# Mixing the two branches of a layer in place in the PSUM banks, on one core

## The chip, the cores and the metric

One core of one Trainium2 chip runs the whole program in one launch. The metric is the device time of an execution in microseconds (us); of several runs the median is given. TensorE is the matmul engine (PE), VectorE is DVE, ScalarE is ACT, GpSimd is POOL, and SyncE (SP) issues most DMAs.

## The reference, cut to what matters

The program is two transformer-like blocks of two layers each, on 512 tokens of width 1024, in fp32. Only the first block is touched. In each of its two layers the outputs of an attention branch and of a gated delta-rule branch are mixed with two gates and sent through one more projection:

```python
y_attn = grid_attention(qa, ka, va) @ w_o_attn[l]
...
y_dn = o.reshape(b, s, DN_V).astype(x.dtype) @ w_o_dn[l]
gates = jax.nn.sigmoid(gate_logit).reshape(b, s, N_BRANCH, D_MODEL)
mixed = gates[:, :, 0] * y_attn + gates[:, :, 1] * y_dn
x = x + (mixed @ w_out[l]).astype(x.dtype)
h = rmsnorm(x, norm_ffn_g[l])
```

## The kernel before, in words

Activations lie transposed: a tile is 128 channels by 512 tokens, and a matrix of width 1024 is 8 such tiles (KB = 8). A product is computed by `gemm_pe` (line 310) in output tiles, one PSUM bank each, banks 0 to 3 in turn, so a product of 8 output tiles takes two turns. fp32 accuracy comes from three matmuls per pair of blocks (lines 343 to 345): weight high part times activation high part, weight high times activation low, weight low times activation high. The high part is the value rounded to the narrower format, the low part is the rest. So each activation tile has to be split in two before TensorE may read it: ACT writes the high part (`h_hi_act`, line 458), DVE subtracts it from the value for the low part (`h_lo_dve`, line 461). The weights are split by POOL (`split_weights`, lines 294 and 296), four slabs in flight (`SLOTS`), each slab being the weights of one output tile. SP (`gemm_sp`, line 228) loads the next slab of a slot when the bank that used the slot is full, by the semaphore `bank_full`. TensorE waits for a slab by `slab_split` and for its bank by `bank_free`.

The order of the work is written out by hand: each engine has its own list, and semaphores join them. With `late=True` the first turn of a product is staggered (line 321): all but the last two activation tiles for output tile 0, then the same for output tile 1, then the last two for both, then output tiles 2 and 3 whole. With `ready` given, TensorE waits ahead of activation tile k of output tile 0 until its low part is there (line 340).

The stage that the change touches is `gates_pe`, `gates_act` and `gates_dve` (lines 1676 to 1738). It has two products back to back:

- the delta branch's output projection: 8 output tiles, each from 4 activation tiles (12 matmuls per bank)
- the projection by `w_out`: 8 output tiles, each from 8 activation tiles (24 matmuls per bank), whose input is the mixed tiles

Between them stands the mixing. The gated output of the attention branch already lies in `H` (8 tiles in SBUF, multiplied by its gate on POOL, line 1666). ACT has turned the delta gates into sigmoids in `ARENA`, tiles 10 to 17 (line 1713). DVE then takes each bank k of the first product as it becomes full: it multiplies it by the gate into the SBUF tile `KF` and frees the bank (line 1732), then adds `KF` to tile k of `H` (line 1735). ACT writes the high part of each finished `H` tile. Only after all 8 tiles does DVE write the 8 low parts into `H_LO` (`h_lo_dve`, line 463). The second product waits for these, tile by tile. Behind it stands `model_dve` (line 465), which adds each bank to `X` (line 483) and prepares the next product.

These lines say the order that matters:

```python
                    nc.vector.tensor_tensor(KF[:], BANK[nb][:], A(i * 4 + (10 + nb)), MUL
                                            ).then_inc(bank_free[nb], 1)
                    dve.wait_ge(bank_free[nb], need(bank_free[nb]))
                    nc.vector.tensor_tensor(blk(H, i * 4 + nb), blk(H, i * 4 + nb), KF[:], ADD).then_inc(mixed_ready, 1)
                    dve.wait_ge(mixed_ready, need(mixed_ready))
            for k in range(KB):
                h_lo_dve(dve, k, tile_of(H_LO), mixed_hi)
```

Of the kernel before, what the change touches and what calls it, by code (L numbers as in the profile page):

```python
# [17 lines left out]
KB = D_MODEL // P  # L18
# [44 lines left out]
def build(nc, w_k8, w_k12, w_k10, xT, memT, par, cst, even, odd, outT, scratch, gate_rows, x_rows):  # L63
    F, R = mybir.dt.float32, mybir.dt.float32r
    ALU, ACT, AX = mybir.AluOpType, mybir.ActivationFunctionType, mybir.AxisListType
    MUL, ADD, SUB = ALU.mult, ALU.add, ALU.subtract
    ctx = ExitStack()
    with ctx:
        def sb(name, shape, dtype=F):
            return ctx.enter_context(nc.sbuf_tensor(name, shape, dtype))  # L70

        def views(*parts):

            with ExitStack() as shared:
                return [shared.enter_context(nc.sbuf_tensor(name, [P, n], R)) for name, n in parts]
# [5 lines left out]
        H_LO, = views(("H_LO", KB * SEQ))  # L81
        H = sb("H", [P, KB * SEQ])
# [12 lines left out]
        QF, KF, VF = sb("QF", [P, SEQ]), sb("KF", [P, SEQ]), sb("VF", [P, SEQ])  # L95
# [16 lines left out]
        BANK = [PSUM[:, b * SEQ:(b + 1) * SEQ] for b in range(8)]  # L112

        def A(i, n=SEQ):
            return ARENA[:, bass.ds(i * SEQ, n)]

        def blk(t, i, n=SEQ, w=SEQ):
            return t[:, bass.ds(i * w, n)]
# [26 lines left out]
        h_hi, h_split = sem("h_hi"), sem("h_split")  # L145
        bank_full = [sem(f"bank_full{b}") for b in range(4)]
        bank_free = [sem(f"bank_free{b}") for b in range(4)]
        squares_added, out_done = sem("squares_added"), sem("out_done")
        sq_done, ss_done, rt_done = sem("sq_done"), sem("ss_done"), sem("rt_done")
        dve_step, act_step, pool_step = sem("dve_step"), sem("act_step"), sem("pool_step")  # L150
# [7 lines left out]
        mixed_ready = sem("mixed_ready")  # L158
# [8 lines left out]
        attn_gates, dn_gates = sem("attn_gates"), sem("delta_gates")  # L167
# [37 lines left out]
        taken = {}  # L205
# [104 lines left out]
        def gemm_pe(pe, slabs, rhs, kb=KB, n=SEQ, halves=False, ready=None, between=None, norm=False, late=False):  # L310

            need = need_pe
            base = need.seen.get(ready.name, 0) if ready is not None else 0

            def parts_of(s):
                return [(s, 2 * (s % 2), 0, kb // 2), (s, 2 * (s % 2) + 1, kb // 2, kb)] if halves else [(s, s, 0, kb)]

            def staggered():
                head = [(s, 2 * s, 0, kb // 2) if halves else (s, s, 0, kb - 2) for s in range(2)]
                tail = [(s, 2 * s + 1, kb // 2, kb) if halves else (s, s, kb - 2, kb) for s in range(2)]
                return head + tail

            def turn(count, between=None, norm=False, late=False):
                order = (staggered() if late else []) + [part for s in range(2 if late else 0, count) for part in parts_of(s)]
                for s, b, k0, k1 in order:
                    first = 0 if not halves or b % 2 == 0 else kb // 2
                    if k0 == 0:  # L330
                        pe.wait_ge(slab_split[s], need(slab_split[s]))
                        need.skip(slab_in[s], 16)
                    if k0 == first:
                        pe.wait_ge(bank_free[b], need(bank_free[b]))
                    out = BANK[b][:, 0:n]
                    final = kb // 2 if halves and b % 2 == 0 else kb
                    for k in range(k0, k1):
                        w_hi, w_lo = (t[s][:, k * P:(k + 1) * P] for t in (W_HI, W_LO))
                        if s == 0 and ready is not None:
                            pe.wait_ge(ready, base + k + 1)  # L340
                        if s == 0 and norm and k == kb - 1:
                            model_sums_pe(pe)
                        mm(out, w_hi, rhs[0](k), start=k == first, stop=False)  # L343
                        mm(out, w_hi, rhs[1](k), start=False, stop=False)  # L344
                        last = mm(out, w_lo, rhs[0](k), start=False, stop=k == final - 1)  # L345
                    if k1 == final:
                        last.then_inc(bank_full[b], 1)
                    if k1 == kb:
                        if s == 1 and norm:
                            model_rows_pe(pe)  # L350
                        if between is not None:
                            between(s)

            per = {bank_free[b]: 2 if halves else 1 for b in range(4)} | {slab_in[s]: 16 for s in range(SLOTS)} | \
                {slab_split[s]: 1 for s in range(SLOTS)}
            whole = slabs // SLOTS
            if between is not None:
                for first in range(0, whole * SLOTS, SLOTS):
                    turn(SLOTS, lambda s: between(first + s), norm and first == 0)
            else:  # L360
                if norm or late or whole == 1:
                    turn(SLOTS, norm=norm, late=late)
                    whole -= 1
                if whole:
                    with need.loop(pe, whole, per):
                        turn(SLOTS)
                turn(slabs % SLOTS)
            if ready is not None:
                need.skip(ready, kb)

        def rhs_of(t, n=SEQ, first=0):
            return lambda k: t[:, (first + k) * n:(first + k + 1) * n]
# [85 lines left out]
        def h_hi_act(k, hi, x=None):  # L458
            nc.scalar.activation(hi(k), x(k) if x else blk(H, k), ACT.Copy).then_inc(h_hi, 1)

        def h_lo_dve(dve, k, lo, hi, x=None):
            dve.wait_ge(h_hi, need_dve(h_hi))
            nc.vector.tensor_tensor(lo(k), x(k) if x else blk(H, k), hi(k).bitcast(F), SUB).then_inc(h_split, 1)  # L463
# [49 lines left out]
        def tile_of(t):  # L513
            return lambda k: blk(t, k)
# [519 lines left out]
        delta_l = [None]  # L1034
# [641 lines left out]
        def gates_pe(pe):  # L1676
            need = need_pe
            taken[f"gates{delta_l[0]}"] = [need.seen[bank_free[b].name] + 1 for b in range(4)]
            gemm_pe(pe, 8, (lambda k: branch_hi(4 + k), lambda k: branch_lo(4 + k)), kb=4, ready=h_split, late=True)
            gemm_pe(pe, 8, (mixed_hi, rhs_of(H_LO)), ready=h_split, late=True)  # L1680
            taken[f"out{delta_l[0]}"] = [need.seen[bank_free[b].name] + 1 for b in range(4)]

        def gates_back_sp(sp, l):
# [15 lines left out]
        def branch_hi(k):  # L1699
            return blk(H_LO2, k)  # L1700

        def mixed_hi(k):
            return blk(ACT_HI, 10 + k) if k < 2 else blk(ACT_LO, k - 2)

        def branch_lo(k):
            return blk(ACT_HI, k if k < 4 else 2 + k)

        def gates_act(act):
            for k in range(4, KB):
                h_hi_act(k, branch_hi, branch)  # L1710
            for i in range(4):
                act.wait_ge(gate_in[i], 16 * (delta_l[0] + 1))
                nc.scalar.activation(A(10 + 2 * i, 2 * SEQ), A(10 + 2 * i, 2 * SEQ), ACT.Sigmoid).then_inc(dn_gates, 1)
            skip_banks(need_act, 2)
            for k in range(KB):
                act.wait_ge(mixed_ready, need_act(mixed_ready))
                h_hi_act(k, mixed_hi)
            skip_banks(need_act, 2)

        def gates_dve(dve, l):  # L1720
            need = need_dve
            for k in range(4, KB):
                h_lo_dve(dve, k, branch_lo, branch_hi, branch)
            banks_taken(dve, need, f"gates{l}")
            dve.wait_ge(*nth("gated", 1))
            per = {bank_full[b]: 1 for b in range(4)} | {bank_free[b]: 1 for b in range(4)} | {mixed_ready: 4, dn_gates: 2}
            with need.loop(dve, 2, per) as i:
                for nb in range(4):
                    dve.wait_ge(bank_full[nb], need(bank_full[nb]))
                    if nb % 2 == 0:  # L1730
                        dve.wait_ge(dn_gates, need(dn_gates))
                    nc.vector.tensor_tensor(KF[:], BANK[nb][:], A(i * 4 + (10 + nb)), MUL
                                            ).then_inc(bank_free[nb], 1)
                    dve.wait_ge(bank_free[nb], need(bank_free[nb]))
                    nc.vector.tensor_tensor(blk(H, i * 4 + nb), blk(H, i * 4 + nb), KF[:], ADD).then_inc(mixed_ready, 1)
                    dve.wait_ge(mixed_ready, need(mixed_ready))
            for k in range(KB):
                h_lo_dve(dve, k, tile_of(H_LO), mixed_hi)


        GT, UP = [QF, KF], [VF, KTOK]
# [1591 lines left out]
```

## Time and profile before

| what | value |
|---|---|
| median of 3 runs | 3731.81 us (3726.59 to 3734.32) |
| the profiled execution's own time | 3725.19 us |
| its span, first to last instruction | 3723.4 us |
| mean granted TensorE clock over the span | 0.975 of full |
| busy: PE, POOL, DVE, ACT | 3585.1, 1818.3, 1694.3, 986.7 us |

The times in the rows further down are microseconds from the start of the span, of one execution. A row of the timeline gives start, duration, engine, line, operation, output and inputs, count, and in brackets how long the engine had been idle and whose result ended that. Matmuls are pipelined, so a row's duration is longer than the distance to the next start; it is the distance that counts. The granted clock is 1.00 at full speed (2.4 GHz) and 0.50 at the lower level (1.2 GHz).

### The profile page before, as it was taken

What the parts mean: (1) busy time and instruction counts of PE and PEld (TensorE: products, weight loads), DVE (VectorE), ACT (ScalarE), POOL (GpSimd) and SP (SyncE); (2) the same over time, 40 slices, a digit from 0 to 9 for tenths busy, and PEclk for the clock granted to TensorE, in tenths of its full rate; (3) what the DMA queues carried; (4) which work ended last, traced back from release to release, by engine and by line L of the source; (5) the groups of instructions that cost most, each with busy time, mean ns of one, the idle gap of its engine ahead of it and who ended that gap; (6) DMA issues with size and microseconds to landing.
All of it is one profiled execution on the core that took longest, in us unless ns stands there. A gap on an engine that the chain in (4) does not pass through costs nothing.

```text
span 3723.4 us, 49812 instructions
## 1 busy us (share of the span) xinstructions
PE 3585.1 (96%) x18732; PEld 2866.8 (77%) x18732; DVE 1694.3 (46%) x2646; ACT 986.7 (26%) x1742; POOL 1818.3 (49%) x1057
## 2 busy tenths in 40 slices
PE   7999889999999989999999999999999999999999
PEld 5777667878776767787878788888887789888887
DVE  5255645637434573573651254344344124344342
ACT  3235532201223464221111233232111124232010
POOL 5522335656553223666666433535656431435654
PEclk9999899999999989999999999999999999999999
DMA  3221022323222101222222311212223423213222
GB/s 117 90 71 32 13 79 81 103 78 98 87 96 97 52 1 58 90 96 91 96 91 92 100 41 52 80 60 93 100 90 102 102 85 97 79 51 96 96 90 91
DMA packets 84152, 299.18 MB, mean 80 GB/s; under 512 B 8600, under 2 KB 9752, under 8 KB 83608
## 3 DMA queue, kind: packets, MB, share of 16 engines
q1 hardware_dynamic: 81904, 290.11, 23.9%
q10 hardware_dynamic: 1032, 2.62, 0.6%
q0 software_dynamic: 1056, 4.19, 0.4%
q8 instruction: 115, 1.88, 0.2%
q14 instruction: 45, 0.37, 0.0%
HBM read 285.88 MB, written 11.01 MB: 80 GB/s over the span
## 4 chain that ended last, share of the span: by engine, by line
PE 80%; DVE 9%; ACT 4%; issue 3%; DMA 2%; POOL 1%; DVEq 0%; ACTq 0%; SPq 0%; POOLq 0%
PE PSUM L345 19%; PE PSUM L344 19%; PE PSUM L343 19%; PE PSUM L904 2%; PE PSUM L1929 1%; PE PSUM L905 1%; PE PSUM L906 1%; PE PSUM L1933 1%; DVE PSUM L502 1%; DMA SLABS<-w_k 1%; PE PSUM L959 1%; DVE ACT_HI L1820 1%; PE PSUM L1501 1%; PE PSUM L916 1%; PE PSUM L1409 1%
## 5 line engine op out<-in xcount | busy, mean ns | idle before, releaser
L296 POOL TENSOR_TENSOR W_LOS<-SLABS,W_HI 128x1024 fp32r<-128x1024 f32 (+3 forms) x454 | 1142.1, 2516 | 37.9
L294 POOL TENSOR_SCALAR W_HI<-SLABS 128x1024 fp32r<-128x1024 f32 (+3 forms) x454 | 507.6, 1118 | 1299.7 <-DMA SLABS<-w_k 1299.6
L344 PE MATMUL PSUM<-H_LO,W_HI 128*128 128x512 f32 x2480 | 984.5, 397 | 0.0
L343 PE MATMUL PSUM<-H_HI,W_HI 128*128 128x512 f32 x2224 | 883.4, 397 | 27.9 <-DVE H_LO L487 22.0
L345 PE MATMUL PSUM<-H_HI,W_LOS 128*128 128x512 f32 x2224 | 884.7, 398 | 0.0
L344 PEld LDWEIGHTS PSUM<-H_LO,W_HI 128*128 128x128 f32 x2480 | 469.0, 189 | 118.1 <-issue 2.4
L343 PEld LDWEIGHTS PSUM<-H_HI,W_HI 128*128 128x128 f32 x2224 | 419.0, 188 | 133.1 <-issue 21.9
L345 PEld LDWEIGHTS PSUM<-H_HI,W_LOS 128*128 128x128 f32 x2224 | 418.7, 188 | 98.7
L502 DVE TENSOR_TENSOR PSUM<-PSUM,FACTORS 128x512 f32<-128x512 f32 x282 | 195.2, 695 | 555.8 <-PE PSUM L345 493.4
L343 PE MATMUL PSUM<-ACT_HI,W_HI 128*128 128x512 f32 x928 | 370.9, 400 | 19.0 <-DVE H_LO L463 12.3
L345 PE MATMUL PSUM<-ACT_HI,W_LOS 128*128 128x512 f32 x928 | 372.0, 401 | 0.0
L344 PE MATMUL PSUM<-ACT_LO,W_HI 128*128 128x512 f32 x896 | 356.6, 398 | 0.0
L343 PEld LDWEIGHTS PSUM<-ACT_HI,W_HI 128*128 128x128 f32 x928 | 176.4, 190 | 63.5 <-issue 11.0
L345 PEld LDWEIGHTS PSUM<-ACT_HI,W_LOS 128*128 128x128 f32 x928 | 176.6, 190 | 41.9
L344 PEld LDWEIGHTS PSUM<-ACT_LO,W_HI 128*128 128x128 f32 x896 | 169.8, 190 | 42.9 <-issue 0.2
L483 DVE TENSOR_TENSOR X<-PSUM,X 128x512 f32<-128x512 f32 x72 | 49.7, 690 | 208.7 <-PE PSUM L345 208.7
L410 DVE TENSOR_TENSOR X<-PSUM,X 128x512 f32<-128x512 f32 x40 | 27.6, 691 | 248.3 <-PE PSUM L345 248.3
L431 ACT ACTIVATE H_HI<-X,PARAM 128x512 fp32r<-128x512 f32 x64 | 45.6, 723 | 267.7 <-DVE X L483 267.7
L904 PE MATMUL PSUM<-H_HI,W_HI 128*128 128x512 f32 x256 | 108.5, 424 | 0.0
L1801 DVE SCALAR_TENSOR_TENSOR QF<-PSUM,PARAM,QF 128x511 f32<-128x511 f32 (+1 forms) x88 | 65.9, 749 | 88.2 <-ACT QF L1771 42.5
L906 PE MATMUL PSUM<-H_HI,W_LOS 128*128 128x512 f32 x256 | 102.7, 401 | 0.0
L905 PE MATMUL PSUM<-H_LO,W_HI 128*128 128x512 f32 x256 | 102.5, 400 | 0.0
(503 smaller groups left out, 5003.2 us busy)
## 6 DMA issues: line engine op xcount, KB each, us to landing
SLABS<-w_k SPq DMA_DIRECT2D x406, 512.0 KB, 3.5
SLABS<-w_k SPq DMA_DIRECT2D x32, 768.0 KB, 4.2
SLABS<-w_k SPq DMA_DIRECT2D x32, 640.0 KB, 3.9
X<-xT SPq DMA_DIRECT2D x2, 2048.0 KB, 9.7
X<-w_k SPq DMA_DIRECT2D x2, 2048.0 KB, 9.1
SLABS<-w_k SPq DMA_DIRECT2D x16, 256.0 KB, 3.2
ARENA<-gate_rows SPq DMA_DIRECT2D x8, 512.0 KB, 5.2
bias_rows<-SQ ACTq DMA_DIRECT2D x1, 2560.0 KB
```

The source lines that it names most:

```text
L294: nc.gpsimd.tensor_scalar(hi, raw, 1.0, 0.0, MUL, ADD).then_inc(pool_step, 1)
L296: nc.gpsimd.tensor_tensor(lo, raw, hi.bitcast(F), SUB).then_inc(slab_split[s], 1)
L343: mm(out, w_hi, rhs[0](k), start=k == first, stop=False)
L344: mm(out, w_hi, rhs[1](k), start=False, stop=False)
L345: last = mm(out, w_lo, rhs[0](k), start=False, stop=k == final - 1)
L431: nc.scalar.activation(hi(k), blk(X, k), ACT.Copy, scale=G(gain, k)).then_inc(h_hi, 1)
L483: nc.vector.tensor_tensor(xb, BANK[k % 4][:], xb, ADD).then_inc(bank_free[k % 4], 1)
L502: nc.vector.tensor_tensor(BANK[b][:], BANK[b][:], FACTORS[:], MUL).then_inc(scaled, 1)
L904: mm(BANK[b][:], hi, blk(H_HI, i), start=i == 0, stop=False)
L905: mm(BANK[b][:], hi, blk(H_LO2, i), start=False, stop=False)
L906: last = mm(BANK[b][:], lo, blk(H_HI, i), start=False, stop=i == KB - 1)
L1801: last = nc.vector.scalar_tensor_tensor(buf[:, lo:hi], BANK[b][:, lo + o:hi + o], G(conv, col), buf[:, lo:hi], MUL, ADD)
```

## The change

The mixing is done in place in the PSUM bank, and the low part of a tile is written by DVE one tile behind, out of the bank, inside the same list. The bank is freed by the low part and no longer by the gate product. TensorE's wait ahead of each activation tile of the second product is on the `bank_free` count that the low part raises, not on `h_split`. ACT reads the high part out of the bank. `KF` is no longer used here, the mixed tiles are no longer written to `H`, and DVE's loop of two turns is unrolled into 8 tiles. DMAs, weights, matmuls and their order are the same.

```diff
@@ gemm_pe
-            base = need.seen.get(ready.name, 0) if ready is not None else 0
+            base = need.seen.get(ready.name, 0) if ready is not None and not callable(ready) else 0
...
-                        if s == 0 and ready is not None:
+                        if s == 0 and callable(ready):
+                            pe.wait_ge(*ready(k))
+                        elif s == 0 and ready is not None:
                             pe.wait_ge(ready, base + k + 1)
...
-            if ready is not None:
+            if ready is not None and not callable(ready):
                 need.skip(ready, kb)
@@ gates_pe
-            gemm_pe(pe, 8, (mixed_hi, rhs_of(H_LO)), ready=h_split, late=True)
+            gemm_pe(pe, 8, (mixed_hi, rhs_of(H_LO)), ready=mixed_split, late=True)
@@
+        def mixed_split(k):
+            return bank_free[k % 4], taken[f"gates{delta_l[0]}"][k % 4] + 1 + k // 4
+
@@ gates_act
-                h_hi_act(k, mixed_hi)
+                h_hi_act(k, mixed_hi, lambda k: BANK[k % 4][:])
@@ gates_dve
-            per = {bank_full[b]: 1 for b in range(4)} | {bank_free[b]: 1 for b in range(4)} | {mixed_ready: 4, dn_gates: 2}
-            with need.loop(dve, 2, per) as i:
-                for nb in range(4):
-                    dve.wait_ge(bank_full[nb], need(bank_full[nb]))
-                    if nb % 2 == 0:
-                        dve.wait_ge(dn_gates, need(dn_gates))
-                    nc.vector.tensor_tensor(KF[:], BANK[nb][:], A(i * 4 + (10 + nb)), MUL
-                                            ).then_inc(bank_free[nb], 1)
-                    dve.wait_ge(bank_free[nb], need(bank_free[nb]))
-                    nc.vector.tensor_tensor(blk(H, i * 4 + nb), blk(H, i * 4 + nb), KF[:], ADD).then_inc(mixed_ready, 1)
-                    dve.wait_ge(mixed_ready, need(mixed_ready))
+
+            def low(k):
+                dve.wait_ge(h_hi, need(h_hi))
+                nc.vector.tensor_tensor(blk(H_LO, k), BANK[k % 4][:], mixed_hi(k).bitcast(F), SUB).then_inc(bank_free[k % 4], 1)
+
             for k in range(KB):
-                h_lo_dve(dve, k, tile_of(H_LO), mixed_hi)
+                bank = BANK[k % 4][:]
+                dve.wait_ge(bank_full[k % 4], need(bank_full[k % 4]))
+                if k % 2 == 0:
+                    dve.wait_ge(dn_gates, need(dn_gates))
+                nc.vector.tensor_tensor(bank, bank, A(10 + k), MUL).then_inc(dve_step, 1)
+                dve.wait_ge(dve_step, need(dve_step))
+                nc.vector.tensor_tensor(bank, bank, blk(H, k), ADD).then_inc(mixed_ready, 1)
+                if k:
+                    low(k - 1)
+            low(KB - 1)
+            for b in range(4):
+                need.seen[bank_free[b].name] = taken[f"gates{l}"][b] + 2
```

## Rows read from the trace of the kernel before

**Rows 1.** The page: span, busy time by engine, and the chain's shares by engine.

```profile
span 3723.4 us, 49812 instructions
PE 3585.1 (96%) x18732; PEld 2866.8 (77%) x18732; DVE 1694.3 (46%) x2646; ACT 986.7 (26%) x1742; POOL 1818.3 (49%) x1057
PE 80%; DVE 9%; ACT 4%; issue 3%; DMA 2%; POOL 1%; DVEq 0%; ACTq 0%; SPq 0%; POOLq 0%
```

**Rows 2.** TensorE's waits, whole span: total us, times, longest us.

```profile
PE PSUM L343 <- DVE H_LO L463: 14.6, 6, 5.1
```

**Rows 3.** Timeline of TensorE at the seam of the two products, layer 0.

```profile
545.95 0.40 PE L345 MATMUL PSUM<-H_LO,W_LOS 128*128 128x512 f32 x1
...
550.85 0.40 PE L345 MATMUL PSUM<-H_LO,W_LOS 128*128 128x512 f32 x1
556.33 0.77 PE L343 MATMUL PSUM<-ACT_HI,W_HI 128*128 128x512 f32 x1 [5.09 <-DVE H_LO L463]
...
567.23 0.45 PE L343 MATMUL PSUM<-ACT_HI,W_HI 128*128 128x512 f32 x1
567.52 0.40 PE L344 MATMUL PSUM<-H_LO,W_HI 128*128 128x512 f32 x1
```

**Rows 4.** Timeline of TensorE at the same seam, layer 1.

```profile
1505.89 0.40 PE L345 MATMUL PSUM<-H_LO,W_LOS 128*128 128x512 f32 x1
1511.43 0.77 PE L343 MATMUL PSUM<-ACT_HI,W_HI 128*128 128x512 f32 x1 [5.14 <-DVE H_LO L463]
...
1523.37 0.39 PE L343 MATMUL PSUM<-ACT_HI,W_HI 128*128 128x512 f32 x1
```

**Rows 5.** The chain of waits in that stretch, layer 0: start, us, what.

```profile
551.40 0.70 DVE KF L1732
552.24 2.52 DVE H L1735
554.95 8.23 DVE H_LO L463 x4
```

**Rows 6.** Busy time by stretch: PE, PEld, DVE, ACT, POOL, granted clock, DMA.

```profile
544.00:551.00 7.00, 7.00 (x32) 5.49 (x30) 4.61 (x5) 1.37 (x3) 6.83 (x6) 1.00 0.64 201
...
551.00:567.00 16.00, 8.73 (x20) 5.50 (x19) 13.82 (x10) 2.65 (x4) 11.38 (x6) 0.58 0.12 41
...
567.00:615.00 48.00, 48.00 (x204) 37.98 (x203) 22.88 (x25) 10.07 (x16) 28.37 (x16) 1.00 0.28 88
```

**Rows 7.** The three DVE operations of the mixing: ns min/median/max, both layers.

```profile
L1732 DVE TENSOR_TENSOR KF<-PSUM,ARENA x16: 690/692/693, 532.8 to 1506.4; 128x512 f32<-128x512 f32 x16
L1735 DVE TENSOR_TENSOR H<-H,KF x16: 692/1103/2550, 533.6 to 1507.3; 128x512 f32 x16
L463 DVE TENSOR_TENSOR H_LO<-H,ACT_LO x12: 676/678/2851, 558.9 to 1520.0; 128x512 fp32r<-128x512 f32 x12
```

**Rows 8.** Operations elsewhere with a PSUM operand: ns min/median/max.

```profile
L502 DVE TENSOR_TENSOR PSUM<-PSUM,FACTORS x282: 683/698/700, 41.4 to 3653.7; 128x512 f32<-128x512 f32 x141
L483 DVE TENSOR_TENSOR X<-PSUM,X x72: 680/692/692, 573.2 to 3342.9; 128x512 f32<-128x512 f32 x72
L442 ACT ACTIVATE FACTORS<-PSUM x10: 597/598/601, 40.6 to 3356.7; 128x512 f32<-128x512 f32 x10
```

**Rows 9.** Timeline of POOL: low parts of the second product's first weight slabs.

```profile
547.61 2.71 POOL L296 TENSOR_TENSOR W_LOS<-SLABS,W_HI 128x1024 fp32r<-128x1024 f32 x1
...
551.86 2.34 POOL L296 TENSOR_TENSOR W_LOS<-SLABS,W_HI 128x1024 fp32r<-128x1024 f32 x1
...
555.73 2.67 POOL L296 TENSOR_TENSOR W_LOS<-SLABS,W_HI 128x1024 fp32r<-128x1024 f32 x1
...
1502.70 2.71 POOL L296 TENSOR_TENSOR W_LOS<-SLABS,W_HI 128x1024 fp32r<-128x1024 f32 x1
```

**Rows 10.** Timeline of DVE and of ACT at the first mixed tile, layer 0.

```profile
528.57 3.90 ACT L1713 ACTIVATE ARENA<-ARENA 128x1024 f32<-128x1024 f32 x4
...
532.78 0.69 DVE L1732 TENSOR_TENSOR KF<-PSUM,ARENA 128x512 f32<-128x512 f32 x1 [4.49 <-PE PSUM L345]
```

## The prediction

> **What bounds the kernel now.** I began with the page: TensorE is busy 3585.1 of 3723.4 us and holds 80% of the chain that ended last [rows 1]. So time comes off only where TensorE stands still or runs slowly, and the question for any edit of DVE's or ACT's work is whether TensorE waits for it. The list of TensorE's waits says yes: it waited 6 times, 14.6 us in all, 5.1 us at the longest, for the low parts of line 463, the form that the change moves [rows 2].
>
> Then the timeline at the seam of the two products. In steady state TensorE starts 21 matmuls between 545.95 and 550.85, which is 4.90 / 21 = 0.2333 us for one [rows 3]. The last matmul of the first product starts at 550.85, so the next could start at 551.09. It starts at 556.33, released by the low part of tile 0 [rows 3]. The chain shows what lies between: gate product 0.70 us, addition 2.52 us, then four low parts in 8.23 us, of which TensorE takes each as it comes [rows 5]. And there is a second loss behind the wait: the granted clock was 1.00 up to the seam, 0.58 from 551 to 567 and 1.00 after it [rows 6]. The clock is at the full level before TensorE stands still, falls towards the lower one (1.2 GHz) with it, and comes back only when 18 matmuls have gone.
>
> **What this costs, step by step.** Layer 0: the 20th matmul of the second product starts at 567.52 [rows 3]. Without wait and at full rate it would start at 551.09 + 19 x 0.2333 = 555.52. The difference is 12.0 us: 5.24 of standing still ahead of the first matmul, 10.90 for the first 18 where 4.20 would do (6.70), and 0.06 at the last. Layer 1: the last matmul of the first product is at 1505.89, the next could be at 1506.13; the 22nd of the second product starts at 1523.37 [rows 4], and could start at 1506.13 + 21 x 0.2333 = 1511.03. The difference is 12.3 us. Together 24.3 us is all that this seam holds.
>
> **What the change does, part by part.**
>
> *The low parts move into the tile's own turn.* DVE then has three operations per tile: gate product, addition, low part of the tile before. Their prices: the gate product today reads PSUM and one SBUF tile and takes 690 to 693 ns in all 16 cases [rows 7]. Written back into the bank, its nearest row is line 502, PSUM from PSUM and SBUF, 698 ns (683 to 700, 282 times) [rows 8]. The in-place addition has these same kinds of operands, 698 ns. The low part becomes SBUF from PSUM and one SBUF tile, the form of line 483 and of today's gate product, 692 ns [rows 7, 8]. From the start of a gate product to the addition that needs it there is 0.84 us (551.40 to 552.24) [rows 5]; the other two follow without a fresh result to wait for. A tile costs 0.84 + 0.70 + 0.69 = about 2.2 us. TensorE fills a bank in 12 x 0.2333 = 2.8 us. DVE keeps up, and its low parts hide beside the matmuls of the next bank.
>
> *These prices have an upper bound in today's rows.* The addition of line 1735 has two SBUF inputs and takes 692 ns at best, 1103 in the middle, 2550 at worst; the low parts 676 to 2851 [rows 7]. In 551 to 567, where they are slow, POOL is busy 11.38 of 16 us with the weights [rows 6]. The gate product, with one SBUF input, never left 693 ns in the same stage. After the change no DVE operation of this stage has two SBUF inputs. I take the low end, because operands and place match; the high end is in a rival. The Trainium skill has a rule for it (SBUF — State Buffer, "Who interferes with whom"): a DVE instruction with two SBUF inputs contends with a GpSimd instruction that reads SBUF, one with at most one SBUF input doesn't. The rows so far agree, and by that rule the high end can't come.
>
> *A rule that speaks against it.* Reading PSUM instead of SBUF, the row with two SBUF inputs is 676 ns at its best and the one with PSUM 690: 14 ns [rows 7]. The Trainium skill (VectorE: DVE Perf Modes, the section on the TRN2 errata) gives a VectorE operation 58 cycles of fixed cost from SBUF and 120 from PSUM, 65 ns more at its 0.96 GHz. By it two moved reads would cost a tile 0.13 us, by the rows 0.03.
>
> *How much room there is.* Call T the time that DVE takes per tile. The first bank is taken at 532.78 [rows 10], and low part k ends behind addition k+1, so at the earliest at 532.78 + (k+2) T. TensorE wants bank 0 for the second product at 551.09, which now needs low part 4: 6 T must be under 18.3, T under 3.05. The waits for the first product's second turn and for tile 5 give about the same (3.1 or more). 2.2 is well inside.
>
> *The tail after the last bank.* Bank 3 is full for tile 7 at about 551.4 [rows 5]. Product, addition, low part 6, low part 7 end at 551.4 + 0.84 + 0.70 + 0.69 + 0.69 = 554.3. TensorE begins the second product at once with tiles 0 to 5 of two outputs, 36 matmuls or 8.4 us, so it wants tile 6 at 559.5. It is there 6 us early. ACT's high part out of the bank costs 598 ns by line 442 [rows 8], less than one DVE operation, and low part k follows it by a whole tile; for tile 7 it runs beside low part 6.
>
> *ACT's queue.* DVE now waits for ACT's high part of tile 0 inside the loop, with all later gate products queued behind. ACT has four sigmoids ahead of it, which end at 532.47, before the first bank is taken at 532.78 [rows 10]. Costed at nothing; were they x late, x - 3 us would show.
>
> *The bank is freed later*, by the low part of the tile, some 2.5 us more than now. A bank comes round after three others, 8.4 us. Nothing.
>
> *The weights are wanted 12 us earlier.* Nothing in SP's or POOL's list moves, and slab loads hang on banks of the first product, so they keep their times. Slab 0 is split at 550.32 and wanted at 551.09; slab 1 at 554.20, wanted after 18 matmuls at 555.3; slab 2 at 558.40, wanted after 48 at 562.3; in layer 1 slab 0 is ready at 1505.41 and wanted at 1506.13 [rows 9, 4]. Margins of 0.7 to 4 us, thin for slab 0 and 1, and they would grow if POOL's splits lose their contention with DVE. This is what is late next.
>
> *Behind the seam* TensorE is busy 48.00 of 48 us [rows 6]: what is gained is passed on and not waited away.
>
> **Sum.** 12.0 + 12.3 = 24.3 us off the profiled execution's 3725.19 (span 3723.4 [rows 1]): 3700.9. That execution lies 6.6 us under the median shown, and 1.4 under its lowest run. Off the median: 3731.8 - 24.3 = 3707.5 us. Clear of 0.2% (7.5 us), which is about what a measurement of this kernel can tell from no change.
>
> **The rivals.**
>
> *A, the weights bound it.* Slab 0 or 1 comes a little late, TensorE waits 1 to 2 us per layer. For: margins of 0.7 and 0.8 us. Against: POOL is helped, if anything. Gain about 20, time 3711.5. 8%.
>
> *B, the slow operations stay slow in their usual size.* T = 0.84 + 1.10 (median of line 1735 [rows 7]) + 2.06 (8.23 / 4 [rows 5]) = 4.0. Tile 5 ends at 532.78 + 7 x 4.0 = 560.8, three more matmuls, and the first 18 are done at 561.5, not at 555.3 and not at today's 567.2. About 5 us per layer remain: 3721.8. Against: the constant 690 to 693 ns beside a busy POOL. 5%.
>
> *C, slower.* Place: the three operations now stand between a full bank and its release, where only the fast gate product stood. If both the addition and the low part took their worst row, T = 0.84 + 2.55 + 2.85 = 6.24 [rows 7], tile 5 ends at 576.5 and the 18 matmuls at 577.2, 10 us behind today's 567.2; twice, 3751.8. It decides from 532.78 + 7 T + 0.7 = 567.2, T = 4.8, where every operation would take over double its row (1.6 us). Against: 282 in-place cases at 700 ns or less [rows 8]. 3%.
>
> *D, nothing gained.* The low parts still come last in effect, because DVE is held early by ACT's list, and TensorE stands as before: 3731.8. Against: 0.3 us in hand even ahead of the first product. 2%.
>
> **The numbers.** The forecast has 82%. Faster holds it, A and B: 95%. Same is D, 2%. Slower is C, 3%. The range 3700 to 3716 holds the forecast with the spread of the runs (about 4 us to each side around the median) and A; it leaves out B, C and D, 10%, and some tails.
>
> **What would show it.** In the profile of the changed kernel: the 14.6 us wait for line 463's output is gone and nothing in its place over 1 us; gate product, addition and low part each at 0.69 to 0.70 us; the granted clock near 1.00 across the seam; the second product's first matmul 0.23 us behind the first product's last. A wait for W_LOS there would be A. Additions or low parts of 1 us and more beside POOL would be B or C. The prediction is wrong if TensorE still stands at the seam, or if later waits grow by what was gained.

## The result

The changed kernel takes 3701.23 us (median of 11 runs, 3694.67 to 3715.98) against 3731.81 (median of 11 runs, 3720.16 to 3738.69): ratio 0.9923, 95% interval 0.9909 to 0.9936. By the ratio that is 28.7 us less, between 23.9 and 34.0 (the two medians by themselves differ by 30.6). The measured time lies in the forecast's range of 3700 to 3716, close to its lower end. The 24.3 us forecast are a ratio of 0.9935, inside the interval but close to its edge: the change gave somewhat more than forecast, if anything. The profiled execution took 3705.52 us, with a span of 3703.7.

First the list of TensorE's waits over the whole span (total us, times, longest), the rows that answer to [rows 2]. The wait for the mixing's low parts, 14.6 us before, isn't in it any more. The first rows of what is left, and the row that the text comes back to:

```profile
PE PSUM L345 <- DVE H_LO L489: 20.9, 4, 18.1
PE PSUM L1454 <- ACT SLABS L1298: 18.0, 6, 4.9
PE PSUM L2039 <- DVE WORK L2294: 10.2, 5, 7.4
...
PE PSUM L345 <- DVE ACT_LO L1832: 8.1, 2, 4.2
```

TensorE's timeline at the seam, layer 0, as in [rows 3]. The second product's first matmul stands 0.23 us behind the first product's last, and its 20th follows 4.44 us later, at full rate:

```profile
544.47 0.40 PE L347 MATMUL PSUM<-H_LO,W_LOS 128*128 128x512 f32 x1
544.70 0.39 PE L345 MATMUL PSUM<-ACT_HI,W_HI 128*128 128x512 f32 x1
...
549.14 0.40 PE L346 MATMUL PSUM<-H_LO,W_HI 128*128 128x512 f32 x1
```

Busy time by stretch, up to the seam and behind it (PE, PEld, DVE, ACT, POOL, granted clock, DMA), as in [rows 6]. TensorE is busy 16.00 of 16 us where it was 8.73, and the granted clock is 1.00 where it was 0.58:

```profile
538.00:545.00 7.00, 7.00 (x32) 5.63 (x31) 4.60 (x8) 1.77 (x3) 5.26 (x5) 1.00 0.64 212
544.50:560.50 16.00, 16.00 (x70) 12.90 (x69) 6.06 (x8) 4.58 (x7) 11.79 (x8) 1.00 0.34 109
```

The three DVE operations of a tile (ns min/median/max, both layers), as in [rows 7]. None takes more than 0.70 us, with POOL busy beside them:

```profile
L1741 DVE TENSOR_TENSOR PSUM<-PSUM,ARENA x16: 689/700/700, 526.9 to 1490.4; 128x512 f32<-128x512 f32 x16
L1743 DVE TENSOR_TENSOR PSUM<-PSUM,H x16: 699/700/700, 527.6 to 1491.1; 128x512 f32<-128x512 f32 x16
L1734 DVE TENSOR_TENSOR H_LO<-PSUM,ACT_LO x12: 679/681/693, 535.0 to 1492.5; 128x512 fp32r<-128x512 f32 x12
```

The tail after the last bank on DVE's timeline. The last two low parts are done at 547.70, and TensorE wants tile 6 only 36 matmuls into the second product, at 544.70 + 8.4 = 553.1:

```profile
544.90 0.70 DVE L1741 TENSOR_TENSOR PSUM<-PSUM,ARENA 128x512 f32<-128x512 f32 x1 [0.78 <-PE PSUM L347]
545.64 0.70 DVE L1743 TENSOR_TENSOR PSUM<-PSUM,H 128x512 f32<-128x512 f32 x1
546.25 1.45 DVE L1734 TENSOR_TENSOR H_LO<-PSUM,ACT_LO 128x512 fp32r<-128x512 f32 x2
```

POOL's timeline, low parts of the second product's first two weight slabs, as in [rows 9]. Slab 0 is ready at 543.77, 0.93 us ahead of its use (0.77 would have been left by the times of before), slab 1 at 547.27, 1.6 us ahead of the 19th matmul. Each split is down to 2.40 us from up to 2.71:

```profile
541.37 2.40 POOL L296 TENSOR_TENSOR W_LOS<-SLABS,W_HI 128x1024 fp32r<-128x1024 f32 x1
...
544.87 2.40 POOL L296 TENSOR_TENSOR W_LOS<-SLABS,W_HI 128x1024 fp32r<-128x1024 f32 x1
```

One thing in the two profiles doesn't fit at first. The spans differ by 19.7 us only, less than the seams alone should give, and the difference isn't made at the seams alone. The changed kernel begins the first product of layer 0 at 520.68 and the one before at 526.63, 5.9 us apart with the same instructions ahead of it. The stretch up to there, before first and changed second (same columns), has 3255 matmuls in both; the mean granted clock was 0.94 in the one and 0.97 in the other.

```profile
0.00:527.00 527.00, 477.88 (x3255) 360.41 (x3256) 264.67 (x515) 212.15 (x411) 196.23 (x129) 0.94 0.20 65
```

```profile
0.00:521.00 521.00, 469.90 (x3255) 351.93 (x3256) 264.75 (x515) 212.25 (x411) 196.34 (x129) 0.97 0.20 66
```

And elsewhere the changed kernel lost ground: 3.1 us between the layer-0 FFN and the first product of layer 1, 5.0 us in the layer-1 FFN, which took 378.2 us (from one scaling row to the next) against 373.2, and 3.6 us in all that follows. In the layer-1 FFN a wait of TensorE for the last low part was 0.7 us before and 3.9 after. Whether that is something given back or chance is what the first experiments had to say.

### The profile page after: what moved, and what is told of

It reads as the page before. It is cut to its first block, busy times and chain, and to the rows that moved or that the text cites. A ratio compares the mean times of both kernels' runs of the same rounds, so it can differ in the third digit from the quotient of the medians.

```text
span 3703.7 us, 49734 instructions
## 1 busy us (share of the span) xinstructions
PE 3574.8 (97%) x18732; PEld 2859.8 (77%) x18732; DVE 1674.7 (45%) x2646; ACT 986.4 (27%) x1742; POOL 1810.1 (49%) x1057
## 3 DMA queue, kind: packets, MB, share of 16 engines
q1 hardware_dynamic: 81904, 290.11, 24.3%
## 4 chain that ended last, share of the span: by engine, by line
PE 80%; DVE 10%; ACT 4%; issue 4%; DMA 1%; DVEq 0%; POOL 0%; ACTq 0%; SPq 0%; POOLq 0%
PE PSUM L346 19%; PE PSUM L347 19%; PE PSUM L345 19%; PE PSUM L906 2%; PE PSUM L1939 1%; PE PSUM L907 1%; PE PSUM L908 1%; PE PSUM L1943 1%; DVE PSUM L504 1%; DVE SLABS L1567 1%; DVE OUTER_PRODUCT L1564 1%; PE PSUM L961 1%; PE PSUM L1503 1%; DVE ACT_HI L1830 1%; PE PSUM L918 1%
```

## The experiments

My theory: the seam held 12.0 and 12.3 us, all of it is gone, because DVE's low parts are now done beside the matmuls. Rivals: the PSUM residence is what does it, by ending the contention with POOL; part is given back in the FFN; a stall costs its own length alone.

**The changed kernel again**, no edit, twice.

> The changed kernel once more, timed in five rounds against the one before. My theory: the seam between the two products held 12.0 us in layer 0 and 12.3 in layer 1, and all of it is gone, so the gain is 24.3 us plus up to 1 us from weight splits that no longer contend: 0.9932 to 0.9936 of the time before. Rival (something else helps too, beside the seam): the first measurement's 0.9923 is right and stays, 28 us or more. Rival (given back): the profiled execution's 19.7 us is the real size, because the middle of the layer-1 FFN waits 3.9 us where it waited 0.7 before. Then that wait should again be near 4 us in layer 1 in this profile, and the ratio 0.9947.

> The changed kernel beside the next one, on one chip. The seam of the mixing should again lose nothing (under 0.1 us per layer), and the two block-1 FFN stretches take 378 to 379 us each, or 373 where the wait in their middle happens to be short. Ratio to the kernel before 0.992 to 0.9935.

Measured: 3705.45 us, ratio 0.9918 (0.9894 to 0.9943), and the second time 3710.72, ratio 0.9939 (0.9918 to 0.9959). The three measurements of this change all hold 0.9935, so an excess over the seam's 24.3 us is not shown. The 0.9947 of the rival that something is given back lies outside the first two intervals and inside the third. But the wait that this rival asked for is there: in the layer-1 FFN it is about 4 us again in both profiles, and the stretch takes 378.9 and 378.2 us. In all three profiles the seam loses under 0.1 us per layer.

**The kernel before again**, no edit, for its profile.

> The kernel before, one more profile, to see what differs between executions of one program. If the wait in the middle of the layer-1 FFN is chance, it may now be 4 us instead of 0.7; the seam should again lose 12.0 and 12.3 us, within 0.3; and the start of the first product should scatter by some us with the granted clock of the stages ahead of it.

Its time was 3736.57 us, its span 3734.7. The seam lost 12.3 and 12.4 us (as worked out in the prediction, from the last matmul of the first product). The waits of TensorE in it, and then the FFN wait in the first profile of before:

```profile
PE PSUM L343 <- DVE H_LO L463: 14.8, 6, 5.2
PE PSUM L343 <- DVE ACT_LO L1822: 7.9, 2, 4.2
```

```profile
PE PSUM L343 <- DVE ACT_LO L1822: 5.0, 2, 4.3
```

So the same program waits 5.0 us in one execution and 7.9 in another: the short and the long form are not made by the change alone. Each number is the sum of a wait in layer 0, about 4 us every time, and one in layer 1, about 4 or about 0.6. Over the ten profiles that kept the FFN as it was (the runs further down among them), the sum is 4.4 to 5.0 us four times and 7.8 to 8.5 six times, on both sides of the change. They are not spread evenly, though. The five profiles in which TensorE has no stop at the seam to speak of (the changed kernel three times, the order alone, one more operation) all have the long form; of the five in which it stops there (before twice, the place alone, the wait put back, three more operations), four have the short one. That can be chance in ten profiles, and it can mean that some 5 us are often given back in the layer-1 FFN. The runs don't decide it. Either way a difference of 5 us can't be read from single profiles of this kernel: the seam has to be read by itself.

**Only the order**, all of it in SBUF as before.

```diff
-            with need.loop(dve, 2, per) as i:
-                for nb in range(4):
...
+            for k in range(KB):
+                dve.wait_ge(bank_full[k % 4], need(bank_full[k % 4]))
...
+                nc.vector.tensor_tensor(KF[:], BANK[k % 4][:], A(10 + k), MUL).then_inc(bank_free[k % 4], 1)
+                dve.wait_ge(bank_free[k % 4], need(bank_free[k % 4]))
+                nc.vector.tensor_tensor(blk(H, k), blk(H, k), KF[:], ADD).then_inc(mixed_ready, 1)
+                dve.wait_ge(mixed_ready, need(mixed_ready))
+                if k:
+                    h_lo_dve(dve, k - 1, tile_of(H_LO), mixed_hi)
+            h_lo_dve(dve, KB - 1, tile_of(H_LO), mixed_hi)
```

> Only the order is changed: low part one tile behind inside the loop, but product into KF, addition into H and low part out of H, all in SBUF as before, bank freed by the product. If the contention with the weight splits is what matters (two SBUF inputs), the addition and low parts keep 0.7 to 2.8 us each and DVE takes T = 0.84 + 1.2 + 1.3 = about 3.4 us per tile against 2.8 for a bank; tile 5 is then late by about 2 us and some of the clock goes too: gain 14 to 20 us, 3712 to 3718. If the order alone does it all: gain 24, as the full change. If the PSUM side is what does it: gain under 8.

Measured: 3707.71 us, ratio 0.9919 (0.9893 to 0.9945), no different from the full change measured beside it (0.9918). My expectation of 14 to 20 us was wrong: the order alone does it. The slow operations are there, in DVE's timeline, for the last two tiles of layer 0 (gate product L1730, addition L1732, and L463 for the last three low parts):

```profile
540.76 0.68 DVE L1730 TENSOR_TENSOR KF<-PSUM,ARENA 128x512 f32<-128x512 f32 x1
541.47 2.17 DVE L1732 TENSOR_TENSOR H<-H,KF 128x512 f32<-128x512 f32 x1
543.68 1.41 DVE L463 TENSOR_TENSOR H_LO<-H,ACT_LO 128x512 fp32r<-128x512 f32 x1
545.01 0.68 DVE L1730 TENSOR_TENSOR KF<-PSUM,ARENA 128x512 f32<-128x512 f32 x1
545.73 2.17 DVE L1732 TENSOR_TENSOR H<-H,KF 128x512 f32<-128x512 f32 x1
547.93 4.21 DVE L463 TENSOR_TENSOR H_LO<-H,ACT_LO 128x512 fp32r<-128x512 f32 x2
```

and yet TensorE goes almost straight on. It starts 0.12 us late, since POOL's split of slab 0 ends only at 543.09, and layer 0 loses 0.27 us at its seam in all; layer 1 loses nothing:

```profile
542.80 0.40 PE L345 MATMUL PSUM<-H_LO,W_LOS 128*128 128x512 f32 x1
543.15 0.50 PE L343 MATMUL PSUM<-ACT_HI,W_HI 128*128 128x512 f32 x1
```

A tile takes DVE 4.25 us here (540.76 to 545.01), but only the last ones do; the four before took 2.72 to 3.12. The last low part is done at 552.14, and the matmul that needs it, with 39 ahead of it in the second product, starts at 552.40, at its usual distance. The room was under 0.3 us, but there was room. The in-place form buys the slack, not the time: in the changed kernel the last low part is done at 547.70 and TensorE uses it at 553.80, 6.1 us later.

**Only the place**: the product is left in the bank and the addition reads it there and writes `H`, the low parts still come last. The addition frees the bank, and ACT's wait ahead of each high part goes by that.

```diff
-                    nc.vector.tensor_tensor(KF[:], BANK[nb][:], A(i * 4 + (10 + nb)), MUL
+                nc.vector.tensor_tensor(bank, bank, A(10 + k), MUL).then_inc(dve_step, 1)
+                dve.wait_ge(dve_step, need(dve_step))
+                nc.vector.tensor_tensor(blk(H, k), bank, blk(H, k), ADD).then_inc(bank_free[k % 4], 1)
+                dve.wait_ge(bank_free[k % 4], need(bank_free[k % 4]))
...
             for k in range(KB):
                 h_lo_dve(dve, k, tile_of(H_LO), mixed_hi)
```

> Only the place of product and addition is changed: product in place in the bank, addition from bank and H into H (one SBUF input), bank freed by it; the eight low parts still come last, out of H with two SBUF inputs. Expected by my theory: the addition falls to 0.70 us everywhere, so the last one no longer takes 2.5 us and the stall before the second product shrinks by 1.8 us per layer, from 5.2 to about 3.4; the low parts still take 0.7 to 2.8 us, TensorE still runs its first matmuls at the lower clock. Gain 3 to 6 us. Rival (the place alone does most of it): gain over 12.

Measured: 3727.27 us, ratio 0.9978 (0.9965 to 0.9990), 8.2 us less. TensorE's timeline at the seam:

```profile
549.48 0.40 PE L345 MATMUL PSUM<-H_LO,W_LOS 128*128 128x512 f32 x1
552.78 0.72 PE L343 MATMUL PSUM<-ACT_HI,W_HI 128*128 128x512 f32 x1 [2.91 <-DVE H_LO L463]
```

It stands still for 3.1 us (552.78 - 549.71) where it was 5.2 to 5.4, and the seam loses 8.7 us per layer where it lost 12.0 to 12.4: 6.9 us over both against the first profile of before. That is a little more than the 3 to 6 expected; matmuls 0.4 us apart and more give way to full distance after 6 of them, where before it took 18. The place alone is the smaller part.

**One wait put back** into the changed kernel.

```diff
         def mixed_split(k):
+            k = KB - 1 if k == 0 else k
             return bank_free[k % 4], taken[f"gates{delta_l[0]}"][k % 4] + 1 + k // 4
```

> The changed kernel with one wait put back: ahead of the second product TensorE waits for the last low part instead of the first. By the profile after, that one ends 3.0 us after the last matmul of the first product, so TensorE stands still for about 3.0 us per layer and then has everything it needs. If a stall costs its own length only: 6 us in all over the changed kernel. If the clock falls with it, as in the trace before (6.7 us of 12.0 came from matmuls at the lower level), the cost is up to 3.0 plus 3 to 4 us per layer: 12 to 14 us, and the rows behind the stall are 0.43 us apart instead of 0.23.

Measured: 3716.26 us, ratio 0.9952 (0.9937 to 0.9968); against 0.9918 for the changed kernel measured beside it that is 13 us, with a wide interval. TensorE's timeline is sharper (layer 0):

```profile
545.42 0.40 PE L347 MATMUL PSUM<-H_LO,W_LOS 128*128 128x512 f32 x1
548.79 0.47 PE L345 MATMUL PSUM<-ACT_HI,W_HI 128*128 128x512 f32 x1 [2.97 <-DVE H_LO L1735]
...
549.57 0.39 PE L345 MATMUL PSUM<-ACT_HI,W_HI 128*128 128x512 f32 x1
549.80 0.50 PE L346 MATMUL PSUM<-H_LO,W_HI 128*128 128x512 f32 x1
550.09 0.63 PE L347 MATMUL PSUM<-ACT_HI,W_LOS 128*128 128x512 f32 x1
```

After the stop the next five matmuls start 0.23 to 0.31 us behind one another, and then the distance goes to 0.43: the clock falls only when TensorE is at work again (mean granted clock 0.62 from 549 to 553). In layer 1 the distance is 0.37 and then 0.43 from the first matmul on. The seam loses 4.75 us in both layers all the same, 3.14 of standing still and 1.61 of slow matmuls, so 9.5 us by the trace. This stall costs more than its length; the 3 to 4 us of clock that I had expected were 1.6.

**Useless DVE operations in each tile**, one and three.

```diff
                 nc.vector.tensor_tensor(bank, bank, blk(H, k), ADD).then_inc(mixed_ready, 1)
+                for extra in (QF, VF, KTOK)[:1]:
+                    nc.vector.tensor_tensor(extra[:], BANK[5][:], FACTORS[:], MUL)
```

with `[:3]` in the second kernel.

> The changed kernel with one useless DVE operation per tile (PSUM and one SBUF input, 0.69 us) between addition and low part. Theory: DVE has room up to T = 3.05 us per tile and uses 2.0 to 2.2; with this it uses 2.6 to 2.8. No wait of TensorE at the seam, no change of time (within 2 us). If the room is smaller than I worked out, TensorE waits at the second product's first tiles.

> The same with three useless operations per tile: T = 2.0 + 3 x 0.61 = about 3.85 us. By the rule of the prediction, tile 5 is ready 7 T after the first gate product, so the 18th matmul of the second product ends at first gate product + 7 x 3.85 + 0.7: 5.7 us later than in the changed kernel, per layer. Cost 11 us, and up to 8 more if the clock falls in the gaps: 11 to 19 us over the changed kernel. If instead only work after the last bank counts, it costs 3 x 0.61 = 1.8 us per layer or nothing.

One more: 3705.57 us, ratio 0.9924 (0.9898 to 0.9951), no wait at the seam; the room for a fourth operation per tile is real. Three more: 3710.91 us, ratio 0.9936 (0.9915 to 0.9957), 4.5 us more than with one, which the two intervals don't separate; the trace does. TensorE's timeline in layer 0 and the stretch around it (columns as before):

```profile
543.69 0.47 PE L345 MATMUL PSUM<-H_LO,W_HI 128*128 128x512 f32 x1 [0.69 <-DVE H_LO L1734]
...
547.41 0.47 PE L345 MATMUL PSUM<-H_LO,W_HI 128*128 128x512 f32 x1 [0.69 <-DVE H_LO L1734]
...
551.09 0.47 PE L345 MATMUL PSUM<-ACT_HI,W_HI 128*128 128x512 f32 x1 [0.65 <-issue]
```

```profile
536.00:555.00 19.00, 16.05 (x64) 11.69 (x65) 18.83 (x32) 3.00 (x5) 15.21 (x12) 1.00 0.39 125
```

TensorE now goes in DVE's step: a bank every 3.72 us (543.69 to 547.41), with a gap of some 0.7 us ahead of each. Five gaps and the slower matmuls behind them cost 4.4 us per layer, 8.8 in all by the trace; I had expected 5.7 from a T of 3.85, and with the measured 3.72 the rule gives 4.7. Up to 8 us more for the clock didn't come: it was granted at 1.00 throughout, although TensorE was idle for 2.95 of the 19 us. So the rule for the room holds to 0.3 us, and here gaps that add to 3.9 us cost 4.4, where one stop of 3.1 us cost 4.75.

**A version that is faster still.** The FFN has a similar pattern: the last tile's high and low part are made out of SBUF by DVE operations that take up to 3.5 and 3.8 us beside POOL, and TensorE waits for them in the middle of the stage. In this version, in all four FFN stages, the product is written to its bank and both parts are made from there; a memset of one column signals.

```diff
-                            last.then_inc(bank_free[b], 1)
+                            if b == v:
+                                last.then_inc(dve_step, 1)
+                            else:
+                                last.then_inc(bank_free[b], 1)
                         if not both:
...
-                            nc.vector.tensor_tensor(UP[s][:], BANK[v][:], FACTORS[:], MUL).then_inc(bank_free[v], 1)
+                            nc.vector.tensor_tensor(BANK[v][:], BANK[v][:], FACTORS[:], MUL).then_inc(dve_step, 1)
...
+                        nc.vector.tensor_tensor(BANK[v][:], GT[s][:], UP[s][:] if both else BANK[v][:], MUL).then_inc(dve_step, 1)
...
-                        nc.vector.tensor_copy(hi, UP[s][:]).then_inc(dve_step, 1)
+                        nc.vector.tensor_copy(hi, BANK[v][:]).then_inc(dve_step, 1)
...
-                        nc.vector.tensor_tensor(lo, UP[s][:], hi.bitcast(F), SUB).then_inc(act_ready, 1)
+                        nc.vector.tensor_tensor(lo, BANK[v][:], hi.bitcast(F), SUB).then_inc(bank_free[v], 1)
+                        dve.wait_ge(bank_free[v], need(bank_free[v]))
+                        nc.vector.memset(STAT[:, 60:61], 0.0).then_inc(act_ready, 1)
```

> The same idea carried to the FFN stages (all four): the product of gate and up half is written into its bank, and high and low part are made out of the bank, so the copy and the subtraction have at most one SBUF input; a tiny memset per tile signals. Theory: in the middle and at the end of the FFN TensorE waits for the last low part; the copy takes 0.43 to 3.5 us and the subtraction 0.69 to 3.8 beside the weight splits. Out of the bank both should stay at 0.7. The waits of 3.9 to 4.2 us in block 1 shrink to about 2, with some of the clock loss behind them: 3 to 8 us faster than the changed kernel, 3693 to 3699. Rival (the bank is held longer and the added signal costs as much): same or slower, the bank waits show up in TensorE's list.

> The FFN version again: both block-1 FFN stretches at 372.2 us, 6.6 us shorter than in the changed kernel each, those of block 2 unchanged at 373.6. So 11 to 14 us under the changed kernel of the same call, ratio to the kernel before 0.989. If the first figure was luck, the difference is under 5 us.

Measured: 3693.39 us, ratio to the kernel before 0.9888 (0.9866 to 0.9910), and the second time 3687.45, ratio 0.9881 (0.9850 to 0.9913), where the changed kernel measured beside it had 0.9939. That second time it is 22 us under the changed kernel by the ratios; the first time none was measured beside it, and against the 0.9918 and 0.9923 of other times it is 11 to 13 us. I had expected 3 to 8 us and then 11 to 14. The rows that bound the layer-0 FFN (the scaling factors of one norm and of the next), changed kernel first, FFN version second:

```profile
608.34 0.60 ACT L444 ACTIVATE FACTORS<-PSUM 128x512 f32<-128x512 f32 x1 [5.94 <-PE PSUM L457]
...
987.24 0.60 ACT L444 ACTIVATE FACTORS<-PSUM 128x512 f32<-128x512 f32 x1 [5.94 <-PE PSUM L457]
```

```profile
601.89 0.60 ACT L444 ACTIVATE FACTORS<-PSUM 128x512 f32<-128x512 f32 x1 [5.94 <-PE PSUM L457]
...
974.10 0.60 ACT L444 ACTIVATE FACTORS<-PSUM 128x512 f32<-128x512 f32 x1 [5.94 <-PE PSUM L457]
```

378.9 us against 372.2, and in layer 1 378.2 against 372.2: 6.7 and 6.0 us, 12.7 in all, and the wait for the FFN's low part is gone from TensorE's list. Against the short form of the layer-1 FFN (373.2) it would be 1.0 instead of 6.0. What the second measurement has beyond 12.7 us isn't explained by these rows. The first FFN of block 2 keeps its 373.6 us. The copy and the subtraction (ns min/median/max) now stay at 0.69 us, where the maxima were 3.5 and 3.8; the copy's median was 0.43 or 0.73 and is 0.69 now, so it is the long ones that count:

```profile
L1828 DVE CAST ACT_HI<-PSUM x88: 691/692/693, 611.8 to 3626.0; 128x512 f32 x88
L1830 DVE TENSOR_TENSOR ACT_LO<-PSUM,ACT_HI x88: 691/692/693, 612.6 to 3626.8; 128x512 f32 x88
```

## Why the prediction was right, point by point

- **The seam held 12.0 + 12.3 us, and the change takes it all.** Shown: it loses 0.0 us in both layers of the changed kernel, and 12.3 and 12.4 in the second profile of before. That the whole time moves by this sum is less certain. The measured ratios hold it, but each with some 5 to 10 us to either side, which is as much as the open question of the layer-1 FFN. That the first measurement (28.7) comes near 24.3 says little against a few us given back and as many gained elsewhere.
- **Prices of the three operations, 0.70, 0.70, 0.69.** Measured 0.700, 0.700, 0.681. With one SBUF input, no DVE operation of the mixing is stretched by POOL, and the splits of POOL are shorter too (2.40 us where they were up to 2.71). By the rule on the shared port (the Trainium skill, SBUF — State Buffer, "Who interferes with whom") it had to be so, and the trace agrees. The 65 ns more for PSUM (the Trainium skill, VectorE: DVE Perf Modes, the section on the TRN2 errata) did not show: the low part is 681 ns from PSUM where its SBUF form's median was 678 [rows 7].
- **T = 2.2 us, room up to 3.05.** The first two tiles are 1.34 us apart without a low part, and with one the three operations take about 2.0. One useless operation more is free, three more cost 4.4 us per layer where the rule gives 4.7.
- **The weights come next.** Slab 0 had 0.9 us in hand and slab 1 had 1.6, more than the 0.8 and 1.1 worked out, with POOL's splits shorter. In the order-only kernel, where they weren't, slab 0 was 0.12 us late in layer 0. Rival A was the nearest of the four.
- **Rival B was thought through wrongly.** It took slow operations to mean half the gain. They stayed slow in the order-only kernel, and only 0.27 us was lost: the additions of over 2 us come when POOL works on the slabs of 128x1024, at the last tiles (about 1.1 us beside those of 128x512), and TensorE asks for the last two tiles after 36 matmuls of other work. I had put T = 4.0 on all eight tiles from the rows of the tail. Its sum was off too: 567.2 - 561.5 is 5.7 us gained per layer and 6.2 left, which makes about 3720 and not 3721.8.
- **Rival C (slower) and D (nothing)** find no row that speaks for them.
- **The clock's share was read too high.** The prediction sets 5.24 us of standing still beside 6.70 for the next 18 matmuls, and speaks of the clock for the second part. The 12.0 us are right, but the 6.70 hold two more waits for low parts (kernel before, layer 0):

```profile
559.01 0.80 PE L343 MATMUL PSUM<-ACT_HI,W_HI 128*128 128x512 f32 x1 [1.06 <-DVE H_LO L463]
...
563.23 0.79 PE L343 MATMUL PSUM<-ACT_LO,W_HI 128*128 128x512 f32 x1 [1.13 <-DVE H_LO L463]
```

The three waits add to 7.3 us, so what is left for slow matmuls is 4.7 of the 12.0. That is also why the wait put back cost only 1.6 us of slow matmuls behind a stop of 3.1: it has no waits behind it, and the long distances last for 8 or 9 matmuls. The forecast didn't need the split, since the change removes all of it.

## What to carry to other kernels

Find the place where TensorE goes from one product to a product of its results, and make each tile ready for TensorE in the same turn that finishes it, not in a pass of its own at the end: that alone gave all but 0.3 us of the seam here. Keeping the tile in its PSUM bank is worth having for another reason, that a DVE operation with only one SBUF input isn't held up by POOL's reading; it paid where DVE's last operations are what TensorE waits for, as in the FFN. Price a stall by TensorE's starts until they are back at full distance, not by the wait's own length, and take out the further waits before you put the rest down to the clock.

## What the runs showed that I had not expected

- The speed at the start of the first product differs between executions, with the same 2.34 us wait ahead of it: its 95 distances take 1.5 to 1.6 us over full rate in 16 of the 24 layers profiled (leaving out waits) and 0.07 in the other eight. The fast starts are in both layers and in five different kernels, among them the changed one; none fell to the six layers of the kernel before and of the place alone. Ahead of the first product of layer 0 nothing differs between the kernels, and yet it starts anywhere from 518.9 to 527.2 us, with a mean granted clock up to there of 0.94 in one execution and 0.97 in another. These, with the 5 us of the layer-1 FFN, are parts of the 20 us of scatter between runs that the profiles show; why the clock differs stays open.
- Gaps of 0.7 us ahead of every bank left the clock at 1.00, while one stop of 3.1 us brought it down, in one layer at once and in the other only after five matmuls.
- The layer-1 FFN's middle wait has two forms in one program, about 4 us and about 0.6. In both profiles of the version whose copy and subtraction read the bank, it is gone, and so is the one in layer 0.
